# GpSimd starts the first up-half weight sums of each feed-forward stage one semaphore count earlier

## The reference, cut to what matters

```python
for i in range(DEPTH):                      # DEPTH = 2
    h = rms_norm(x, norm_mix_g[i])
    y = short_conv_mixer(h, ...) if i % 4 == 0 else mla_mixer(h, ...)
    x = x + y
    h = rms_norm(x, norm_ffn_g[i])
    x = x + (silu(h @ w_gate) * (h @ w_up)) @ w_down     # FFN_HIDDEN = 2816
return rms_norm(x, final_norm_g)
```

## Time and profile before

| | before |
|---|---|
| median of 3 runs | 1082.21 us (1081.59 to 1083.25) |
| the profiled execution: time, span | 1081.93 us, 1080.1 us |
| TensorE matmul busy | 1068.1 us (99% of the span) |
| VectorE busy | 811.6 us (75%) |
| ScalarE busy | 473.6 us (44%) |
| GpSimd busy | 225.6 us (21%) |
| mean granted TensorE clock | 0.998 |

### The profile page before, as it was taken

The page is one execution under the profiler, slowest core; times in us unless marked ns, Lnnn a source line. Parts: engine busy times, 40 slices in busy tenths (PEclk is TensorE's granted clock), DMA queues, the critical chain, the costliest instruction groups (busy, mean ns, idle before and its releaser), DMA issues. The chain is left out here.

```text
span 1080.1 us, 18498 instructions
## 1 busy us (share of the span) xinstructions
PE 1068.1 (99%) x6624; PEld 947.2 (88%) x6624; DVE 811.6 (75%) x1113; ACT 473.6 (44%) x698; POOL 225.6 (21%) x209
## 2 busy tenths in 40 slices
PE   9999999999999999999999999999999999999997
PEld 7888888999999998888878766789999999978886
DVE  5755659999999999444557688599999999984343
ACT  6312235644444456222356477465444444542222
POOL 6000001332332320111200355013232233101110
PEclk9999999999999999999999999999999999999999
DMA  7333332233233234333422111113323323333321
GB/s 199 116 89 107 92 103 78 79 117 116 79 116 117 85 99 120 108 95 97 119 82 83 25 32 48 39 40 118 114 81 117 117 80 114 107 107 91 96 66 79
DMA packets 144038, 101.66 MB, mean 94 GB/s; under 512 B 3912, under 2 KB 142336, under 8 KB 144000
## 3 DMA queue, kind: packets, MB, share of 16 engines
q1 hardware_dynamic: 143648, 100.61, 30.5%
q0 software_dynamic: 320, 0.55, 0.2%
q10 hardware_dynamic: 32, 0.01, 0.0%
HBM read 99.06 MB, written 2.10 MB: 94 GB/s over the span
## 5 line engine op out<-in xcount | busy, mean ns | idle before, releaser
L376 PE MATMUL ps<-x_op_hi,op_w_hi 128*128 128x256 f32 x1232 | 349.2, 283 | 0.7 <-DVE op_w_lo L522 0.7
L377 PE MATMUL ps<-x_op_lo,op_w_hi 128*128 128x256 f32 x1232 | 348.6, 283 | 0.0
L378 PE MATMUL ps<-x_op_hi,op_w_lo 128*128 128x256 f32 x1232 | 348.6, 283 | 0.0
L376 PEld LDWEIGHTS ps<-x_op_hi,op_w_hi 128*128 128x128 f32 x1232 | 236.5, 192 | 2.7 <-DVE op_w_lo L522 1.5
L377 PEld LDWEIGHTS ps<-x_op_lo,op_w_hi 128*128 128x128 f32 x1232 | 236.5, 192 | 0.1
L378 PEld LDWEIGHTS ps<-x_op_hi,op_w_lo 128*128 128x128 f32 x1232 | 236.5, 192 | 0.0
L376 PE MATMUL ps<-hid_hi,wgt_hi 128*128 128x512 f32 (+1 forms) x550 | 211.9, 385 | 0.7 <-DVE hid_lo L1116 0.7
L378 PE MATMUL ps<-hid_hi,wgt_lo 128*128 128x512 f32 (+1 forms) x550 | 209.5, 381 | 0.0
L377 PE MATMUL ps<-hid_lo,wgt_hi 128*128 128x512 f32 (+1 forms) x550 | 209.5, 381 | 0.0
L360 DVE TENSOR_TENSOR wgt_lo<-raw,wgt_hi 128x1024 fp32r<-128x1024 f32 (+4 forms) x131 | 137.5, 1067 | 90.8 <-ACT wgt_hi L351 89.2
L351 ACT ACTIVATE wgt_hi<-raw 128x1024 fp32r<-128x1024 f32 (+4 forms) x131 | 106.6, 830 | 142.2 <-PE ps L378 140.6
(11 more groups left out here) (164 smaller groups left out, 1222.4 us busy)
## 6 DMA issues: line engine op xcount, KB each, us to landing
pair_raw<-in_ffn_w_gate SPq DMA_DIRECT2D x22, 1024.0 KB, 5.2
pair_raw<-in_ffn_w_up SPq DMA_DIRECT2D x22, 1024.0 KB, 5.2
raw<-in_conv_w_in SPq DMA_DIRECT2D x24, 512.0 KB, 3.8
raw<-in_ffn_w_down SPq DMA_DIRECT2D x32, 384.0 KB, 3.3
raw<-in_ffn_w_down SPq DMA_DIRECT2D x32, 320.0 KB, 2.9
raw<-in_conv_w_out SPq DMA_DIRECT2D x8, 512.0 KB, 3.6
raw<-in_mla_w_o SPq DMA_DIRECT2D x8, 512.0 KB, 3.9
x_nat<-in_x SPq DMA_DIRECT2D x4, 512.0 KB, 6.8
```

The costliest lines, as they stand in the source:

```text
L376: nc.tensor.matmul(acc, wh, xh, start=first, stop=False)
L377: nc.tensor.matmul(acc, wh, xl, start=False, stop=False)
L378: return nc.tensor.matmul(acc, wl, xh, start=False, stop=last)
```

## The change

One wait of GpSimd is for one count less of `x_op_done`: 11 in stage 0 where it was 12, and 23 in stage 1 where it was 24. The two other conditions of `weight_sums(l, 0, 1)`, the weights loaded and part 1 of the first group split, stay. No instruction is added, removed or moved; the order of the instructions on each engine is the same in both kernels.

```diff
             def ffn(l):
 
-                pool.wait_ge(x_op_done, 12 * (l + 1))
+                pool.wait_ge(x_op_done, 12 * (l + 1) - 1)
                 weight_sums(l, 0, 1)
 
                 with pool.Fori(1, PAIRS_F) as i:
                     for par in range(2):
                         weight_sums(l, i, par)
```

## The result

The changed kernel takes **1084.83 us** (median of 7 runs, 1084.36 to 1087.85) against 1082.21 us before, also 7 runs (1081.59 to 1083.25). The ratio is 1.0031, with a 95% interval of 1.0022 to 1.0041, so it is slower by 0.3%. The forecast was 1084.8 us, with slower as the likeliest. The profiled execution took 1084.54 us with a span of 1082.6, against 1081.93 and 1080.1 before: +2.6 and +2.5 us.

What follows compares the result with a forecast made beforehand. TensorE, busy for 99% of the span, was taken as the bound. Per stage +2.26 at p4, less 0.61 and 0.27 or 0.23, gave +2.8; 0.1 off each made +2.6, forecast 1084.8 us, 8-in-10 range 1082.8 to 1085.9.

Steps and rivals of the forecast that it cites:

- When GpSimd starts: Sum 0 of the up group in stage 0 would start at 191.49 instead of 192.96, some 1.5 us sooner.
- The holds: Each GpSimd sum holds VectorE's next instruction by 1.1 us, now the last x_op_lo write and part 3: part 3 2.22 late.
- the reading that the prediction set beside this one: Exclusive lock for whole instructions of 1.45 us: part 3 held back 2.9 rather than 2.2, total 4.0 instead of 2.6.
- TensorE at p4: After the statistic, p4 starts at 196.34 instead of 194.12, with a slower first matmul: +2.26 us per stage.
- What is given back: TensorE's waits at p1 of the up group go, 0.61 per stage, and later small waits, 0.27 and 0.23.
- the 0.1 taken off: Taken off for each stage, for part of the waits at the start of the down projection, 0.4 over two.
- The late gate load: Next gate weights load 2.2 us later, landing about 201.7; that group's sums then make VectorE some 0.3 us late, covered.
- the 1.6 us of cover: Extra distance of TensorE to VectorE from p1 of the up group on, said to cover the late load's 0.3.
- rival C: Clock falls in TensorE's new 2.0 us gap ahead of p4, half of 5 us lost per stage: +5, 1089.8 us; chance 0.05.
- a granted clock that fell around 196: Sign that the prediction is wrong: the granted clock falling in a stretch around 196, near p4 of stage 0.
- the main sum: Stage 0 +1.38 and stage 1 +1.42, together +2.8, with 0.1 off each: +2.6 us; chance 0.80.
- Rival A: Early sums disturb nothing on the path, ACT begins part 1 sooner, waits at p1 go: -1.7, 1080.5 us; chance 0.04.

Runs made afterwards that it cites:

- run with one sum ahead: Changed kernel with GpSimd's old wait put between the two sums, so only sum 0 starts early: 1082.78 us, ratio 1.0005 to the kernel before.
- the one with one input: Changed kernel with the two sums replaced by one-input GpSimd instructions of 128x512 that don't compute them: 1081.95 us, ratio 0.9998 to the kernel before.
- the repeated run: The changed kernel measured once more with no edit: 1086.29 us, ratio 1.0041 to the kernel before.
- the last two runs: Kernel before with VectorE making the first up group's two sums behind part 3: stage 0 only 1080.53 us; both stages, a repeat, 1079.85 us.

## Why the prediction was right, point by point

**When GpSimd starts.** Forecast 191.49, measured 191.50, and 726.52 in stage 1. (The prediction names 725.2 for stage 1, and 730.05 for p4 there, from its times of before; the delay of stage 0, 1.3 us, comes on top.)

**The holds.** Each of GpSimd's sums kept VectorE's next instruction back by 1.10 and 1.06, forecast 1.1 and 1.09. Part 3 ended 2.17 later, forecast 2.22. The run with one sum ahead (+1.09 at p4) and the one with one input (0.42 each) show by themselves that it is the holds that make p4 late; the first of these shows that the holds count one by one, and the run with stage 0 alone that the stages do. By the whole recorded length of each sum, the reading that the prediction set beside this one, the delay would have been 2.9. The Trainium skill (SBUF — State Buffer, section "SBUF: two separate sides") calls the shared port pair an exclusive lock, and the trace agrees: each sum and VectorE's instruction with two SBUF inputs went one behind the other. The recorded length is not the price of a sum, since in the changed kernel the sums are recorded with 1.67 and 1.77 us and hold 1.1.

The 1.1 holds for the rows that the prediction read, but not everywhere. In the later groups of the kernel before a sum comes while VectorE works on an instruction that reads the accumulator (for instance 200.31 to 200.99, which keeps its 0.68 though the sum starts at 200.56), and goes on beside it; the next one is then held by 0.8 only, and the second sum costs 0.16 (timeline of VectorE; undisturbed 0.68 and 1.22):

```profile
200.91 1.50 DVE L522 TENSOR_TENSOR op_w_lo<-w_sum,op_w_hi 128x512 fp32r<-128x512 f32 x1
...
203.26 1.38 DVE L522 TENSOR_TENSOR op_w_lo<-pair_raw,op_w_hi 128x1024 fp32r<-128x1024 f32 x1
```

**TensorE at p4.** +2.17 instead of +2.26. The restart costs the same as before (second matmul 0.20 after the first, before 0.19), so the +0.04 for it was 0.03 too much, and part 3 makes the other 0.05.

**What is given back.** No wait is left at p1, at 241 or at 754, as forecast. Of the waits at the down projection the first one shrank: the matmul that started 0.60 behind the one ahead of it (422.31) now starts 0.45 behind it (423.49), and the second kept its wait of 0.17. So the 0.1 taken off was about right. Stage 0 came out at +1.19 against 1.28, stage 1 (2.57 - 1.32, from the statistic on) at +1.25 against 1.32.

**The late gate load.** It was meant to make VectorE 0.3 late. It was more. The load landed when GpSimd started, at 202.67, 1.0 later than forecast, and VectorE's rows are

```profile
203.54 2.32 DVE L1188 TENSOR_TENSOR gate_u<-gate_u,inv 128x1024 f32<-128x1024 f32 x1
205.78 1.78 DVE L522 TENSOR_TENSOR op_w_lo<-pair_raw,op_w_hi 128x512 fp32r<-128x512 f32 x1
207.48 0.68 DVE L1036 TENSOR_TENSOR w_sum<-pair_raw 128x512 f32<-128x512 f32 x1
```

Both sums now meet instructions with two SBUF inputs and hold 1.11 (2.32 for 1.21) and 1.10 (1.78 for 0.68), where before they held 0.82 and 0.16. Its `third_sum` for this group starts at 207.48, and 206.30 before: 1.2 late. It stayed covered by TensorE's own lateness, and no wait of TensorE follows, so the result did not move; but the term was wrong, and three quarters of the 1.6 us of cover were used up.

**The clock.** Here the prediction put a rare case at 5% and 5 us. By the groups of times it is a common case, about every second wait of 1.93 us, and costs 1.5 us a wait, where rival C had 2.5; seen directly it was in one of the five such waits in the three traces (the changed kernel twice, stage 0 alone). The prediction named a granted clock that fell around 196 as a sign that it was wrong: at 196 it stayed at 1.00 in these traces, and it fell at the same place of stage 1, at 732, in the repeated run. The forecast of 1084.8 matches the lower group of the changed kernel (mean 1084.61) and also the median of the result, but the latter is luck: four of the first seven runs happened to be in that group. Over all 12 runs the median is 1086.2, 0.3 above the range given. So the mechanism of the main sum was right for executions at full clock, its sum to 0.1 us a stage, and the 1.4 to 1.5 us that a half clock adds were not in it. The Trainium skill (TensorE: Matmul & The Clock Gate, section "Part 1: The HAM clock gate (the "warmup" mystery)") says that the throttled clock is the default and activity releases it; the prediction read in it no reason for a fall after such a short gap. The trace of the repeated run shows such a fall (0.50 in 732 to 734), and the measurement decides. Why it comes behind some waits of the same length and not behind others is open.

**The other side.** Rival A asked that GpSimd's sums disturb nothing on the path, and gave 1080.5. No sum on GpSimd did so; with the sums on VectorE, behind part 3, the same waits went and TensorE ended 1.50 sooner, which fits A's price for them (-1.7). The medians of the last two runs, less the 0.9 at the end, give less: 1.2 for both stages and 0.5 for one, where A's terms make 1.7 and 0.9.

## What to carry to other kernels

Before an instruction of GpSimd with two SBUF inputs is moved earlier, look at which VectorE instruction stands next at the new place and who waits for it: here each such sum of 512 columns took 1.1 us from VectorE where it met only instructions with two SBUF inputs, and 0.8 or less where it found one that reads the accumulator. VectorE makes the same sum itself in 0.7 us, so work that falls on a busy stretch of VectorE need not be saved by giving it to GpSimd. A wait of TensorE can cost more than its length: look at the granted clock behind it in more than one execution, and at whether the run times stand in groups.

## What was not expected of the hardware

- Behind a wait of TensorE of 1.93 us in a kernel that is otherwise 99% busy, the granted clock was at 0.50 until some 3.3 us after the restart, at a cost of 1.5 us, in one of five such waits in the traces, and by the times in about every second one. Behind waits of 0.86 and 0.59 us (11 and 10 runs), and where matmuls without use filled the gap (11 runs), the times show no such group.
- A GpSimd instruction with one input of 512 columns held VectorE's next one by 0.42 us, with two inputs by 1.1, and by 0.8 where VectorE was on an instruction that reads the accumulator when the sum came.
- The last write of the output landed in 3.1 us in the three profiles in which VectorE makes the sums, and in 4.0 in the nine others; the cause is open.
